# Spreading three of every four cache loads over later half blocks of TensorE work in a two-layer hybrid decoder step

## The chip, the cores and the metric

One core of one Trainium2 chip. The metric is the device time of one execution of the kernel in microseconds (us); of several runs the median counts.

## The reference, cut to what matters

Two layers of a hybrid decoder run over a prompt of 256 tokens and over 8 sample sequences of 4 tokens each, 288 token columns in all. Each layer is a half-step feed-forward network, a mixer of three branches with gates, and a second feed-forward network. The part that the change touches is the attention of the sample tokens into their own memory caches, in branch C:

```
x = LN1(alpha*x + 0.5*SwiGLU_1(x))
z = x @ w_in                                   # splits into cv, cb, cc, lx, lg, q and three gates
s = einsum('bthd,bmhd->bhtm', q, k_mem) / sqrt(128)      # sample b has its own k_mem[b], v_mem[b]
o = einsum('bthd,bmhd->bthd', softmax(s), v_mem)         # 256 memory tokens, 4 heads of 128
merged = g0 * (A @ conv_out) + g1 * (B @ lru_out) + g2 * (o @ att_out)
x = LN2(alpha*x + merged @ w_o)
x = LN3(alpha*x + 0.5*SwiGLU_2(x))
```

For each layer there are 8 key caches and 8 value caches, of 512 KB each, in HBM.

## The kernel before, in words

All data is float32. Each weight is cut into blocks of 1024 x 256 (1 MB) or 512 x 256 (512 KB). SyncE loads block n into one half of the buffer `raw` (n mod 2); it may do so when `lo_ready` says that both halves of block n-2 have been split. ScalarE casts the block to its high part `whi` (the helper `hi`, L735, recorded at L733), VectorE computes the rest `wlo` (the helper `lo`, L1036, recorded at L1030), each in two half blocks, and TensorE multiplies three times for each pair of 128-wide tiles (`stream`, L443, recorded at L439 to L441): a block of 1 MB is 48 matmuls of 288 columns, one of 512 KB is 24. After each half of a block TensorE raises `pe_half` by one, so `pe_half` = 2(n+1) says that block n is done.

The order of the work is written out by hand for each engine. The mixer's gated part of a layer is 24 blocks, from block number B on: for each of three branches b and each i of 0 to 3, a gate block `gate(b, i)` (number B+8b+2i, 1 MB out of `w_in`), and then a projection block `project(b, i)` (number B+8b+2i+1, 512 KB out of `conv_out`, `lru_out` or `att_out`).

Between these blocks TensorE does the sample attention in groups of four samples: the scores of samples 0 to 3 stand behind gate(0,1) (block B+2), those of 4 to 7 behind gate(0,3) (B+6), the values of 0 to 3 behind project(1,1) (B+11), those of 4 to 7 behind project(1,3) (B+15). The functions are `sample_scores` (L617, matmul L623) and `sample_values` (L627, matmul L631). Each sample raises `kv_used` by one.

GpSimd (POOL) issues the cache loads. There are four buffers `kv[0]` to `kv[3]`, two of them in the tensor `kv_more` and two within `pool`; load b (0 to 7 keys, 8 to 15 values) goes to buffer b mod 4, and from b = 4 on waits until sample b-4 has been used. The loop also has two other jobs: behind load 3 it clears `qz`, and behind load 11 it waits for the first prompt probabilities (`p_prob`) and clears the two `pz` tiles (L422), into which VectorE then copies the sample probabilities (L1463):

```
for b in range(2 * NS):
    if b == 2:
        pool_e.wait_ge(conv_done, l + 1)
    if b >= BATCH:
        pool_e.wait_ge(kv_used, l * (2 * NS) + b - BATCH + 1)
    ...
    g.dma_start(kv[b % BATCH], cache).then_inc(kv_in[b % BATCH], 16)
```

Other lines that the prediction's steps touch: `gate_lo` (L1375) is VectorE's split of the gate block after the next one; `branch_y` (L1378) drains a projection and splits the projection block after it; L1406, L1410, L1412 and L1413 are steps of the recurrent branch on VectorE; `prompt_values` (L649, matmul L654) needs the prompt probabilities that VectorE copied at L1466, behind the `pz` copies at L1463, and VectorE does these behind `gate_lo(1, 0, 0)`, the split of block B+10. L690 is the transpose of the sample probabilities, right behind gate(1,0).

Of the kernel before, what the change touches and what calls it, by code (L numbers as in the profile page):

```python
# [91 lines left out]
def hybrid_decoder_step(nc, I, O, dims):  # L92
# [20 lines left out]
    plan = Plan(L, KF, KB)  # L113
# [15 lines left out]
    with ExitStack() as ctx:  # L129
# [3 lines left out]
        def sem(name):  # L133
            return ctx.enter_context(nc.semaphore(name))
# [26 lines left out]
        KV, BATCH = AH * M, NS // 2  # L161
# [77 lines left out]
        hi_ready, lo_ready, pe_half, drained = sem("hi_ready"), sem("lo_ready"), sem("pe_half"), sem("drained")  # L239
# [138 lines left out]
        @block.gpsimd  # L378
        def _(pool_e):
            g = nc.gpsimd  # L380
            g.memset(ident[:, :], 0.0).then_inc(consts, 1)
            pool_e.wait_ge(consts, 1)
            g.affine_select(out=ident[:, :], in_=ident[:, :], compare_op=ALU.not_equal, fill=1.0, base=0,
                            pattern=[[-1, P]], channel_multiplier=1).then_inc(consts, 1)
            g.memset(ones[:, :], 1.0 / D).then_inc(consts, 1)
            for i, c in enumerate((4.0, 2.0, 4.0)):
                g.memset(eps[:, i:i + 1], EPS * c * c).then_inc(consts, 1)
            g.memset(junk[:, :], 1.0).then_inc(consts, 1)
            g.memset(bd[:, :, :, :], 0.0).then_inc(bd_zero, 1)
            pool_e.wait_ge(bd_zero, 1)  # L390
            pool_e.wait_ge(x_ready, KD)
            g.dma_start(pts[:, :, :], I["params"]).then_inc(pts_in, 16)

            pool_e.wait_ge(h_ready, 3)
            g.dma_start(sts[:, :, :, :], I["states"]).then_inc(sts_in, 16)
            g.dma_start(mem[:, :, :], I["mem"]).then_inc(mem_in, 16)
            for l in range(L):
                if l > 0:
                    pool_e.wait_ge(bd_psum, l * 8)
                for j, w in enumerate(("lru_wa", "lru_wx")):  # L400
                    for e in range(2):
                        h = P // 2
                        g.dma_start(bd[e * h:(e + 1) * h, j, :, e * h:(e + 1) * h],
                                    I[w][l].rearrange("(k e) a b -> e a k b", e=2)[e]).then_inc(bd_in, 16)
                pool_e.wait_ge(fill_out, plan.fills_done(l, "k"))
                g.dma_start(O["p_mem_k"][l], kt[:, :, :]).then_inc(k_out, 16)
                pool_e.wait_ge(fill_out, plan.fills_done(l, "v"))
                g.dma_start(O["p_mem_v"][l], vt[:, :, :]).then_inc(v_out, 16)

                for b in range(2 * NS):  # L410
                    if b == 2:
                        pool_e.wait_ge(conv_done, l + 1)
                    if b >= BATCH:
                        pool_e.wait_ge(kv_used, l * (2 * NS) + b - BATCH + 1)
                    cache = I["cache_k" if b < NS else "cache_v"][l, b % NS]
                    g.dma_start(kv[b % BATCH], cache).then_inc(kv_in[b % BATCH], 16)
                    if b == BATCH - 1:
                        g.memset(qz_flat, 0.0).then_inc(qz_zero, 1)
                    if b == NS + BATCH - 1:
                        pool_e.wait_ge(p_prob, l * AH + 1)  # L420
                        for t in pz_flat:
                            g.memset(t, 0.0).then_inc(pz_zero, 1)  # L422
                if l + 1 < L:
                    pool_e.wait_ge(kv_used, (l + 1) * (2 * NS))
                    g.dma_start(mem[:, :, :], I["mem"]).then_inc(mem_in, 16)
                pool_e.wait_ge(col_ready, l + 1)
                g.dma_start(O["cols"][l], cols[:, l]).then_inc(col_out, 16)

        @block.tensor
        def _(pe):  # L430
# [25 lines left out]
            def first_blocks(n):  # L456

                for s, k in ((s, k) for s in range(2) for k in range(KD)):
                    if (s, k) == (0, 0):
                        pe.wait_ge(xh_ready, 1)  # L460
                    elif s == 0:
                        pe.wait_ge(x_ready, k + 1)
                    if s == 0 and k % 2 == 0:
                        pe.wait_ge(lo_ready if k % 4 else first_lo, k // 4 + 1)
                    for h, (k0, _) in enumerate(halves(KD)):
                        if s == 1 and k == k0:
                            pe.wait_ge(lo_ready, 2 * (n + s) + h + 1)
                    for t in range(2):
                        out = ps[:, 2 * s + t, 0:T]
                        c = slice(t * P, (t + 1) * P)  # L470
                        mm(out, whi[:, s, k, c], xh[:, k, :], start=k == 0, stop=False)  # L471
                        mm(out, wlo[:, s, k, c], xh[:, k, :], start=False, stop=False)  # L472
                    if (s, k) == (0, 0):
                        pe.wait_ge(x_ready, 1)
                    for t in range(2):
                        last = mm(ps[:, 2 * s + t, 0:T], whi[:, s, k, t * P:(t + 1) * P], xl[:, k, :],
                                  start=False, stop=k == KD - 1)
                    if k in (KD // 2 - 1, KD - 1):
                        last.then_inc(pe_half, 1)
# [1088 lines left out]
```

## Time and profile before

| what | before |
|---|---|
| median of 3 runs | 1396.47 us (1395.02 to 1397.4) |
| the profiled execution's own time | 1396.84 us |
| its span, first to last instruction | 1394.9 us |
| TensorE (PE) busy | 98% of the span |
| VectorE (DVE), ScalarE (ACT), GpSimd (POOL) busy | 64%, 48%, 2% |
| granted TensorE clock | 0.998 |
| DMA | 243.60 MB, mean 175 GB/s |
| cache loads | 32 of 512 KB, on GpSimd's queue |
| loads of gate blocks and others out of `w_in` | 48 of 1 MB on SyncE's queue, 4.9 us median to landing |

A busy share says how much of the span an engine had an instruction running. "Landing" is the time from the issue of a transfer to its semaphore. The span leaves out 1.94 us of the execution's own time, at its two ends.

### The profile page before, as it was taken

What the parts mean: (1) busy time and instruction counts of PE and PEld (TensorE: products, weight loads), DVE (VectorE), ACT (ScalarE), POOL (GpSimd) and SP (SyncE); (2) the same over time, 40 slices, a digit from 0 to 9 for tenths busy, and PEclk for the clock granted to TensorE, in tenths of its full rate; (3) what the DMA queues carried; (4) which work ended last, traced back from release to release, by engine and by line L of the source; (5) the groups of instructions that cost most, each with busy time, mean ns of one, the idle gap of its engine ahead of it and who ended that gap; (6) DMA issues with size and microseconds to landing.
All of it is one profiled execution on the core that took longest, in us unless ns stands there. A gap on an engine that the chain in (4) does not pass through costs nothing.

```text
span 1394.9 us, 25447 instructions
## 1 busy us (share of the span) xinstructions
PE 1373.7 (98%) x10566; PEld 1357.2 (97%) x10566; DVE 894.8 (64%) x1180; ACT 665.9 (48%) x896; POOL 34.8 (2%) x68
## 2 busy tenths in 40 slices
PE   9999999999999999999999999999999999999996
PEld 8999999999899999999999999999998999999996
DVE  5555568496865885554685555585887568655444
ACT  5444446445444664444474444463544455544433
POOL 0100000000101000000000000000001000000000
PEclk9999999999999999999999999999999999999999
DMA  6654444755555454444445544446455453554441
GB/s 241 203 178 157 152 166 160 258 179 178 203 191 204 159 182 157 173 154 162 167 167 181 179 154 143 166 172 228 167 202 204 162 200 129 181 180 153 171 166 57
DMA packets 39998, 243.60 MB, mean 175 GB/s; under 512 B 4577, under 2 KB 4593, under 8 KB 16369
## 3 DMA queue, kind: packets, MB, share of 16 engines
q1 hardware_dynamic: 33264, 219.00, 45.0%
q0 software_dynamic: 5936, 22.01, 4.3%
q10 hardware_dynamic: 720, 1.47, 0.3%
q8 instruction: 59, 0.97, 0.3%
q14 instruction: 19, 0.15, 0.0%
HBM read 238.97 MB, written 3.50 MB: 174 GB/s over the span
## 4 chain that ended last, share of the span: by engine, by line
PE 91%; DVE 4%; DMA 3%; ACT 1%; issue 1%; DVEq 0%
PE ps L440 29%; PE ps L439 29%; PE ps L441 29%; DMA raw<-in_w_in 2%; DVE wlo L1030 1%; PE ps L527 1%; ACT whi L733 1%; PE ps L638 1%; PE ps L631 1%; PE ps L654 1%; PE ps L599 0%; PE ps L623 0%; DMA raw<-in_ffn_wg 0%; PE ps L471 0%; PE ps L472 0%
## 5 line engine op out<-in xcount | busy, mean ns | idle before, releaser
L1030 DVE TENSOR_TENSOR wlo<-raw,whi 128x1024 fp32r<-128x1024 f32 (+1 forms) x450 | 510.1, 1141 | 320.6 <-ACT whi L733 316.4
L733 ACT CAST whi<-raw 128x1024 fp32r<-128x1024 f32 (+1 forms) x446 | 437.2, 987 | 505.1 <-PE ps L441 382.9
L439 PE MATMUL ps<-xh,whi 128*128 128x288 f32 (+1 forms) x2144 | 635.6, 296 | 4.4 <-DVE wlo L1030 3.2
L440 PE MATMUL ps<-xl,whi 128*128 128x288 f32 (+1 forms) x2144 | 631.4, 294 | 0.0
L441 PE MATMUL ps<-xh,wlo 128*128 128x288 f32 (+1 forms) x2144 | 630.5, 294 | 0.0
L439 PEld LDWEIGHTS ps<-xh,whi 128*128 128x128 f32 x2144 | 404.4, 189 | 6.9 <-ACT pool L964 2.9
L440 PEld LDWEIGHTS ps<-xl,whi 128*128 128x128 f32 x2144 | 406.1, 189 | 0.7
L441 PEld LDWEIGHTS ps<-xh,wlo 128*128 128x128 f32 x2144 | 405.5, 189 | 0.0
L439 PE MATMUL ps<-hh,whi 128*128 128x288 f32 (+1 forms) x1088 | 322.0, 296 | 0.0
L440 PE MATMUL ps<-hl,whi 128*128 128x288 f32 (+1 forms) x1088 | 319.4, 294 | 0.0
L441 PE MATMUL ps<-hh,wlo 128*128 128x288 f32 (+1 forms) x1088 | 319.1, 293 | 0.0
L440 PEld LDWEIGHTS ps<-hl,whi 128*128 128x128 f32 x1088 | 206.1, 189 | 0.4
L439 PEld LDWEIGHTS ps<-hh,whi 128*128 128x128 f32 x1088 | 205.2, 189 | 1.2 <-issue 0.8
L441 PEld LDWEIGHTS ps<-hh,wlo 128*128 128x128 f32 x1088 | 205.7, 189 | 0.0
L1100 DVE SCALAR_TENSOR_TENSOR pool<-pool,ps 128x576 f32<-128x576 f32 x41 | 30.9, 753 | 49.9 <-ACT pool L774 49.9
L774 ACT ACTIVATE pool<-ps 128x576 f32<-128x576 f32 x41 | 26.7, 651 | 69.9 <-PE ps L441 69.9
L1106 DVE TENSOR_TENSOR pool<-pool,ps 128x576 f32<-128x576 f32 x44 | 33.1, 753 | 34.6 <-PE ps L441 34.6
L1030 DVE TENSOR_TENSOR hl<-pool,hh 128x576 f32 (+3 forms) x54 | 45.2, 844 | 0.9 <-ACT hh L819 0.2
L1146 DVE SCALAR_TENSOR_TENSOR y<-x,ps 128x576 f32<-128x576 f32 x18 | 13.6, 754 | 33.6 <-PE ps L441 33.6
L791 ACT CAST hh<-pool 128x576 f32 (+1 forms) x44 | 29.7, 675 | 3.2 <-DVE pool L1106 3.2
L860 ACT ACTIVATE xh<-y,pts 128x288 fp32r<-128x288 f32 x40 | 20.4, 532 | 18.9 <-DVE y L1221 18.4
L964 ACT ACTIVATE pool<-ps 128x576 f32<-128x576 f32 x24 | 15.6, 650 | 18.6 <-PE ps L441 18.6
(191 smaller groups left out, 747.5 us busy)
## 6 DMA issues: line engine op xcount, KB each, us to landing
raw<-in_w_in SPq DMA_DIRECT2D x48, 1024.0 KB, 4.9
raw<-in_ffn_wg SPq DMA_DIRECT2D x43, 1024.0 KB, 4.9
raw<-in_ffn_wu SPq DMA_DIRECT2D x43, 1024.0 KB, 4.9
raw<-in_ffn_wd SPq DMA_DIRECT2D x32, 1024.0 KB, 4.9
raw<-in_ffn_wd SPq DMA_DIRECT2D x16, 768.0 KB, 4.1
raw<-in_w_o SPq DMA_DIRECT2D x8, 1024.0 KB, 4.9
raw<-in_w_k_mem SPq DMA_DIRECT2D x4, 1024.0 KB, 5.5
raw<-in_w_v_mem SPq DMA_DIRECT2D x4, 1024.0 KB, 5.7
```

Source lines behind the costliest of these rows:

```text
L439: mm(out, wh, mh, start=start, stop=False)
L440: mm(out, wh, ml, start=False, stop=False)
L441: return mm(out, wl, mh, start=False, stop=stop)
L527: return mm(ps[:, 4 + kind, 0:T], ones[:, :], tile, start=first, stop=last)
L733: s_.copy(whi[:, s, k0:k1, :], raw[:, s, k0:k1, :]).then_inc(hi_ready, 1)
L774: s_.activation(th[:, :, :], ps[:, 0:2, 0:T], ACT.Tanh, scale=0.5).then_inc(ffn_tanh, 1)
L791: s_.copy(hh[:, bass.ds(i * 2, 2), :], hf[:, :, :]).then_inc(ffn_hi, 1)
L860: return s_.activation(out[:, k, :], y[:, k, :], ACT.Identity, bias=pts[:, l, bc + k:bc + k + 1])
L964: s_.activation(tg[:, :, :], ps[:, 0:2, 0:T], ACT.Tanh, scale=0.5).then_inc(gate_tanh, 1)
L1030: return v.tensor_tensor(out, full, high.bitcast(F32), sub)
L1100: v.scalar_tensor_tensor(sg[:, :, :], th[:, :, :], 1.0, ps[:, 0:2, 0:T], add, mult).then_inc(drained, 1)
L1106: v.tensor_tensor(hf[:, :, :], sg[:, :, :], ps[:, 2:4, 0:T], mult).then_inc(drained, 1)
```

## The change

For loads b = 5, 6, 7, 9, 10, 11, 13, 14, 15 of each layer, GpSimd waits for one more condition before it issues the load: that TensorE has reached a certain half block, counted by `pe_half`. Loads 4, 8 and 12 are issued as before. In each group of four the second load waits until the projection block behind the next place is done, the third for half of the gate block after it, the fourth for the other half. Nothing is taken out.

```
+                def spread(b):
+
+                    n = plan.at[l]["B"] + (2, 6, 10)[b // BATCH - 1]
+                    return 2 * n + (0, 4, 5, 6)[b % BATCH]
+
                 for b in range(2 * NS):
                     if b == 2:
                         pool_e.wait_ge(conv_done, l + 1)
                     if b >= BATCH:
                         pool_e.wait_ge(kv_used, l * (2 * NS) + b - BATCH + 1)
+                        if b % BATCH:
+                            pool_e.wait_ge(pe_half, spread(b))
                     cache = I["cache_k" if b < NS else "cache_v"][l, b % NS]
                     g.dma_start(kv[b % BATCH], cache).then_inc(kv_in[b % BATCH], 16)
```

## Rows read from the trace of the kernel before

**Rows 1.** The page: busy time of TensorE, and the chain that ended last.

```profile
PE 1373.7 (98%) x10566; PEld 1357.2 (97%) x10566; DVE 894.8 (64%) x1180; ACT 665.9 (48%) x896; POOL 34.8 (2%) x68
PE 91%; DVE 4%; DMA 3%; ACT 1%; issue 1%; DVEq 0%
```

**Rows 2.** Waits of TensorE, whole span: us in total, times, longest us.

```profile
PE ps L439 <- DVE wlo L1030: 3.2, 2, 2.7
```

**Rows 3.** Chain that ended last, layer 0, from 344 us: start, us, what.

```profile
344.79 7.77 DMA raw<-in_w_in
...
352.58 1.05 ACT whi L733
...
353.73 1.24 DVE wlo L1030
```

**Rows 4.** Timeline of GpSimd, layer 0: start, us, what, idle before and releaser.

```profile
338.68 1.05 POOL L416 DMA_DIRECT2D kv_more<-in_cache_k  x2 [36.73 <-PE ps L623]
...
362.56 1.05 POOL L416 DMA_DIRECT2D kv_more<-in_cache_v  x2 [21.79 <-PE ps L623]
...
373.89 1.84 POOL L422 MEMSET pool<- 128x1024 f32 x2 [9.23 <-DVE pool L1457]
391.82 1.05 POOL L416 DMA_DIRECT2D kv_more<-in_cache_v  x2 [16.09 <-PE ps L631]
```

**Rows 5.** Landing, us, of loads issued at 344.79, 1030.46, 1054.71, 333.31, 369.86.

```profile
raw<-in_w_in SPq DMA_DIRECT2D x1, 1024.0 KB, 7.8
...
raw<-in_w_in SPq DMA_DIRECT2D x1, 1024.0 KB, 6.9
...
raw<-in_w_in SPq DMA_DIRECT2D x1, 1024.0 KB, 6.3
...
raw<-in_w_in SPq DMA_DIRECT2D x1, 1024.0 KB, 6.0
...
raw<-in_w_in SPq DMA_DIRECT2D x1, 1024.0 KB, 4.8
```

**Rows 6.** Timeline of SyncE's queue: the loads of gate blocks B+10 and B+16, layer 0.

```profile
369.86 0.33 SPq L325 DMA_DIRECT2D raw<-in_w_in  x1
...
403.12 0.33 SPq L325 DMA_DIRECT2D raw<-in_w_in  x1
```

**Rows 7.** Stretches: length; PE, PEld, DVE, ACT, POOL busy (count); clock; DMA share; GB/s.

```profile
344.00:352.00 8.00, 8.00 (x64) 8.00 (x63) 7.97 (x8) 0.00 (x0) 0.00 (x0) 1.00 0.79 293
...
362.00:364.00 2.00, 2.00 (x34) 1.14 (x24) 1.63 (x2) 1.78 (x3) 1.44 (x3) 1.00 0.14 51
364.00:366.00 2.00, 2.00 (x15) 1.95 (x14) 1.51 (x5) 0.57 (x2) 0.65 (x2) 1.00 1.03 385
```

**Rows 8.** Timeline of VectorE, layer 0: the steps that bound an early landing.

```profile
351.35 0.81 DVE L1413 TENSOR_SCALAR pool<-pool 128x1248 f32<-128x1248 f32 x1
...
376.91 0.48 DVE L1463 COPY pool<-ps 128x128 f32<-128x128 f32 x2
377.31 0.68 DVE L1466 COPY pool<-ps 128x512 f32<-128x512 f32 x1
```

**Rows 9.** Timeline of TensorE, layer 0: gate(0,2), project(0,3), L690 and prompt_values(0) start.

```profile
342.81 0.29 PE L439 MATMUL ps<-xh,whi 128*128 128x288 f32 x1
...
364.24 0.48 PE L439 MATMUL ps<-hh,whi 128*128 128x288 f32 x1
...
373.92 0.38 PE L690 MATMUL ps<-ident,pool 128*128 128x128 f32 x2
...
378.14 1.10 PE L654 MATMUL ps<-pool,vt 128*128 128x256 f32 x4 [0.22 <-DVE pool L1466]
```

**Rows 10.** Timelines of TensorE and ScalarE, layer 1: the same three places.

```profile
1039.92 0.37 PE L439 MATMUL ps<-xh,whi 128*128 128x288 f32 x1 [0.45 <-DVE wlo L1030]
...
1061.07 1.05 ACT L733 CAST whi<-raw 128x1024 fp32r<-128x1024 f32 x1 [5.83 <-DMA raw<-in_w_in]
...
1064.51 1.10 PE L654 MATMUL ps<-pool,vt 128*128 128x256 f32 x4 [1.72 <-DVE pool L1466]
```

## The prediction

> **What bounds the kernel now.** I read the page first. TensorE is busy 98% of the span and makes up 91% of the chain that ended last [rows 1]. So a change in when GpSimd issues a load can only move the 21 us in which TensorE stands still, and of those only what lies beside cache loads. Next the waits of TensorE: it waited twice for a `wlo` split, 3.2 us in all, once for 2.7 us [rows 2]. The chain tells where: in layer 0 the gate block B+6 was issued at 344.79 and took 7.77 us to arrive; then a cast of 1.05, a split of 1.24 that ended at 354.97, and only then could TensorE start gate(0,3) [rows 3]. Layer 1 has the same wait with 0.45 us [rows 10]. The other waits near the loads are at `prompt_values(0)`: 0.22 us in layer 0 [rows 9], 1.72 in layer 1 [rows 10], behind the split of block B+10.
>
> Then the landings. An undisturbed 1 MB load out of `w_in` takes 4.8 us, B+6 took 7.8 in layer 0 and 6.9 in layer 1, B+10 6.3 in layer 1 and 4.8 in layer 0 [rows 5]. B+4 took 6.0 with no cache load near, so not all lateness comes from these. GpSimd issued four cache loads from 338.68, 362.56 and 391.82 on [rows 4]; after the second of these the queues moved 51 GB/s until 364 and 385 GB/s after it [rows 7]: 0.1 MB, or 0.3 us at the full rate, before 364, so the data starts some 1.2 us after the issue. 512 KB at 385 GB/s is 1.36 us, a group of four some 5.5 to 7 us. The first group flows from about 340 to 347, into the start of B+6's load; the second from 363.7 to about 370.5, just before B+10's, issued at 369.86 [rows 6].
>
> **Where the change puts each load.** Half a gate block is 24 matmuls, as many as a projection block. From gate(0,2)'s start at 342.81 to the split that gate(0,3) waited for (354.97, less 2.7 of waiting) are 72 of them in about 9.5 us [rows 2, 3, 9], so a step is about 3.15 us. project(0,1) ends where gate(0,2) begins. In layer 0:
> Load 4 stays. Load 5 is issued at 342.9 and flows 344.1 to 345.5. Load 6 is issued at 346.0 and flows 347.2 to 348.6. Load 7 is issued at 349.1 and flows 350.3 to 351.7. They are needed behind gate(0,3), two steps after 355, at about 361, so they are in time by over 5 us.
> Load 8 stays. project(0,3) starts at 364.24 [rows 9], so load 9 is issued at 367.5 and flows 368.7 to 370.1; load 10 at 370.7, flowing 371.9 to 373.3; load 11 at 373.9, flowing 375.1 to 376.5. They are needed at about 391, where TensorE frees the first of that group's buffers [rows 4].
> Load 13's condition is already met when load 12's is, because the values of samples 0 to 3 stand behind project(1,1). From 391.82 on [rows 4], loads 14 and 15 come some 5 and 8 us later, at 397 and 400, and flow until about 403, where the next `w_in` load is issued [rows 6]. They are needed two pairs of blocks behind 391.82, six steps or 19 us later, at about 411. I cost this group at nothing in both layers; the cover is some 8 us of slack, and if it went each late us would be one of TensorE.
>
> **B+6, layer 0.** Its load flows from about 346 to 349.3 when nothing is in its way. Now it has the tail of four loads before it; then it has the whole of load 6 in its middle, and load 5 only just ahead. Bounds for its landing: 4.8 us as if alone, or 7.8 as now and, if a whole cache load costs that much again, up to 9.1. I take 4.8 + 1.36 = 6.1, all of one cache load in its way, since the undisturbed row and the price per load are both measured at this place. It lands at 350.9, its cast ends at 352.0. But VectorE is busy for 7.97 of the 8 us to 352 [rows 7] with work that doesn't depend on this load, and its L1413 ends at 352.16 [rows 8]. Only then can the split start, 1.55 us earlier than 353.73. So of 2.73 us of wait, 1.2 stay whatever the load does: **-1.5 us**.
>
> **B+6, layer 1.** The load took 6.9 us for a wait of 0.45; at 6.1 the wait is gone: **-0.45 us**. It can't be more.
>
> **B+10, layer 0.** The second group now lies in a hole of SyncE's queue. After the change load 10 flows within this load's 371 to 374.3: 4.8 + 1.36 = 6.1 us. Behind it on the engines' queues stand ScalarE's cast, VectorE's split, the `pz` copies at 376.91 and the copy L1466, and TensorE waits for that already, by 0.22 us [rows 8, 9]. So all of it shows: **+1.3 us**. Bounds: 0 if the queues share without harm, +3.0 if it lands as late as B+6 does now.
>
> **B+10, layer 1.** It took 6.3 us [rows 5] though the second group was all but through. With load 10 in its way it takes 6.1 if the present lateness was chance, 6.3 + 1.36 if it was not. I take **-0.1 us**, bounds -1.4 (it lands in 4.9) and +1.5 (it lands in 7.8).
>
> **The `pz` clearing.** GpSimd's two memsets stand behind load 11 and now start at 373.89 for 1.84 us [rows 4]. With the change GpSimd waits for the end of gate(1,0) first, just before L690 at 373.92 [rows 9], and issues load 11, half of 1.05 us: the memsets end at about 376.35 instead of 375.73, still 0.55 us before VectorE copies at 376.91. Hidden in both layers; if VectorE came earlier, it would cost at most the 0.6 us of delay in each layer.
>
> Nine more semaphore waits per layer on GpSimd (2% busy) cost nothing. Loads 7 and 11 flow beside the 512 KB projection loads B+7 and B+11; these are used one block later, 6 us on, and 1.36 us more are covered.
>
> **Sum:** -1.5 - 0.45 + 1.3 - 0.1 = -0.75 us. The profiled execution took 1396.84 us, so it would take 1396.1; it stands 0.4 above the median, so I expect a median of 1395.7 us. No change that can be told: about 0.2%, or 2.8 us, is what a measurement of this kernel can tell from none.
>
> The queues' sharing deserves a second look. B+6's load got 3.0 and 2.0 us late from a burst that overlapped only its start [rows 5]. The Trainium skill, "DMA: Bandwidth & Descriptors", section "Queues, rings and completion order", says that each DMA engine takes turns between its queues, packet by packet. By that rule load 10 would give way to half of B+10's packets and cost 0.65 us instead of 1.36, and the sum would be about -2.1 us; the measured lateness of 2 to 3 us is more than taking turns explains.
>
> **Rivals.**
> *Clean sharing, faster.* The lateness came from the bursts' length, and a single 512 KB load hardly hurts. Then B+6 gives 1.55 and 0.45, B+10 in layer 0 costs nothing, and in layer 1 it lands in 4.9 instead of 6.3, giving 1.4: -3.4 us, 1393.1. For it: the only very late loads were beside bursts. Against: B+4 was 6.0 without one, and a MB and a half must pass at about 385 GB/s in any case. The middle way, -2.1 us, still counts as no change. Chance of faster by over 0.2%: 0.10.
> *Collision at B+10, slower.* What makes a load late is any cache load in flight with it, long or short; each costs the 2 to 3 us seen at B+6. Then B+6 gains nothing, B+10 lands in 7.8 in both layers: +3.0 and +1.5, together +4.5 us, 1401.0. It decides from the point where a collision costs more than 2.2 us at each of the two B+10 loads with nothing won at B+6, or less if B+6 gets worse. For it: VectorE's `pz` copies stand behind that split, and the second group was well placed before. Against: B+10 in layer 0 began while the second group's tail was flowing and still landed in 4.8. Chance of slower by over 0.2%: 0.17.
> *The loads don't move.* If the waits were already met, nothing would change and the time were 1396.5. By the block numbers that holds for load 13 alone. It falls within "same" with the forecast, which has 0.73 with it.
>
> **Numbers.** The forecast's own bounds are about -2.1 to +2.5. To leave out no more than 2 in 10, I go to most of the faster rival and to near the slower one: 1392.9 to 1400.0.
>
> **What the changed profile would show.** GpSimd's timeline has single cache loads about 3.1 us apart in the first two groups, and the third as two, one, one. B+6 lands in about 6.1 us in both layers, and VectorE's split for gate(0,3) starts right behind L1413; TensorE's wait there is 1.2 in layer 0 and none in layer 1. B+10 lands in 6.1 us, and `prompt_values(0)` waits about 1.5 us in both. The memsets start about 0.6 us later and nobody waits for them. The prediction is wrong if B+10's landing stays at 4.8 or goes beyond 7, if B+6's does not fall, or if a new wait of over 1 us shows at a place not named here.

## The result, and the profile after

The changed kernel takes 1399.37 us (median of 9 runs, 1398.57 to 1403.48) against 1395.16 us of the kernel before (9 runs). The ratio is 1.0036, with a 95% interval of 1.0026 to 1.0046: slower by 0.36%; the medians are 4.2 us apart. I had forecast no change: the median lies inside my range, but the forecast of no difference was wrong. The profiled execution took 1401.3 us with a span of 1399.3, 4.4 us over that of before. Line numbers above L415 are 7 higher than in the kernel before: L1473 is the old L1466, L661 the old L654.

GpSimd's timeline of the changed kernel, layer 0: start, length, what, count, idle time before and its releaser.

```profile
338.97 0.53 POOL L423 DMA_DIRECT2D kv_more<-in_cache_k  x1 [36.73 <-PE ps L630]
343.82 0.53 POOL L423 DMA_DIRECT2D kv_more<-in_cache_k  x1 [4.33 <-PE ps L448]
346.96 0.53 POOL L423 DMA_DIRECT2D pool<-in_cache_k  x1 [2.60 <-PE ps L448]
350.09 0.53 POOL L423 DMA_DIRECT2D pool<-in_cache_k  x1 [2.61 <-PE ps L448]
362.60 0.53 POOL L423 DMA_DIRECT2D kv_more<-in_cache_v  x1 [11.98 <-PE ps L630]
368.33 0.53 POOL L423 DMA_DIRECT2D kv_more<-in_cache_v  x1 [5.21 <-PE ps L448]
371.46 0.53 POOL L423 DMA_DIRECT2D pool<-in_cache_v  x1 [2.60 <-PE ps L448]
374.60 0.53 POOL L423 DMA_DIRECT2D pool<-in_cache_v  x1 [2.61 <-PE ps L448]
375.12 1.86 POOL L429 MEMSET pool<- 128x1024 f32 x2
```

The change did what it says: where there were bursts of four [rows 4], there are single loads 3.14 us apart, each released by TensorE. Now the waits of TensorE, whole span (total, times, longest):

```profile
PE ps L661 <- DVE pool L1473: 5.5, 2, 3.2
...
PE ps L446 <- DVE wlo L1037: 2.5, 1, 2.5
```

The wait for splits was 3.2 us [rows 2] and is 2.5: of the two only layer 0's is left. The wait at `prompt_values(0)` was 0.22 and 1.72 us [rows 9, 10]; it is 2.24 and 3.22. The landings of the loads of B+6 (issued at 345.21 in layer 0, 1032.52 in layer 1) and B+10 (369.91, 1056.06), in that order:

```profile
raw<-in_w_in SPq DMA_DIRECT2D x1, 1024.0 KB, 7.4
...
raw<-in_w_in SPq DMA_DIRECT2D x1, 1024.0 KB, 4.9
...
raw<-in_w_in SPq DMA_DIRECT2D x1, 1024.0 KB, 6.7
...
raw<-in_w_in SPq DMA_DIRECT2D x1, 1024.0 KB, 7.8
```

Against 7.8, 6.9, 4.8 and 6.3 [rows 5]. The chain that ended last runs through B+10's load in both layers; here is layer 1's (start, length, what):

```profile
1056.06 7.80 DMA raw<-in_w_in
...
1063.88 1.05 ACT whi L740
...
1066.10 0.48 DVE pool L1470 x2
1066.58 0.61 DVE pool L1473
...
1067.33 1.43 PE ps L661 x4
1068.76 1.71 PE ps L645 x4
```

The last two lines are slower than their work: in layer 0 of the same trace they are 1.10 and 0.86. The stretches from 1066 us on (columns as in [rows 7]) say why; the number behind POOL's is TensorE's granted clock:

```profile
1066.00:1068.00 2.00, 0.67 (x3) 0.65 (x4) 2.00 (x5) 1.55 (x3) 0.00 (x0) 0.99 0.07 29
1068.00:1070.00 2.00, 2.00 (x7) 1.56 (x6) 2.00 (x4) 0.37 (x1) 0.00 (x0) 0.50 0.45 74
1070.00:1072.00 2.00, 2.00 (x12) 1.91 (x11) 1.96 (x5) 0.00 (x0) 0.00 (x0) 0.66 0.89 369
```

Behind the wait of 3.22 us the clock was at 1.2 instead of 2.4 GHz for 3.4 us. At half pace that costs an estimated 1.7 us: 7 and 12 matmuls started in two stretches where the following one of this trace has 17. In the mixers of the kernel before the clock is 1.00 throughout.

The 4.4 us between the two spans are thus accounted for: B+6 -0.2 (2.73 to 2.52) and -0.45, B+10 +2.0 and +1.5, clock +1.7, together +4.6.

### The profile page after: what moved, and what is told of

The parts are those of the page before. It is cut to its first block, busy times and chain, and to the rows that moved or that the text cites. A ratio compares the mean times of both kernels' runs of the same rounds, so it can differ in the third digit from the quotient of the medians.

```text
span 1399.3 us, 25465 instructions
## 1 busy us (share of the span) xinstructions
PE 1375.3 (98%) x10566; PEld 1358.6 (97%) x10566; DVE 894.9 (64%) x1180; ACT 666.0 (48%) x896; POOL 35.4 (3%) x68
## 4 chain that ended last, share of the span: by engine, by line
PE 94%; DVE 3%; DMA 1%; issue 1%; ACT 0%; DVEq 0%
PE ps L447 30%; PE ps L446 30%; PE ps L448 30%; DMA raw<-in_w_in 1%; DVE wlo L1037 1%; PE ps L534 1%; PE ps L645 1%; PE ps L606 1%; PE ps L661 1%; PE ps L638 1%; PE ps L630 1%; PE ps L478 0%; DMA raw<-in_ffn_wg 0%; PE ps L479 0%; PE ps L483 0%
```

## The experiments

Theory C: cache loads issued close to B+10's load make it late, and the loss is there. Twelve runs follow: ten kernels, and one more trace of each of the two above. The edits are against the changed kernel unless it says otherwise. "Against before" is the ratio to the kernel before in runs on the same chip, with its 95% interval.

**Group two at once, groups one and three spread** (`e1_group2_at_once`).

```
-                        if b % BATCH:
+                        if b % BATCH and b // BATCH != 2:
```

> The changed kernel, but loads 9, 10 and 11 are issued at once as before; groups one and three stay spread. Theory C (collision): the 3.6 us of new waiting at prompt_values(0) come from cache loads issued around the load of gate block B+10. Then B+10 lands in 4.8 to 6.3 us again in both layers, the wait at the matmul of prompt_values falls from 5.5 us to about 1.9 or less, and the time is at or some 0.5 to 2 us under the kernel before. Rival R (the lateness of B+10 is chance, or the extra waits themselves cost time): B+10 lands in 6.7 and 7.8 as in the changed kernel and the time stays 3 to 5 us above the kernel before.

Measured: 1.0017 (1.0007 to 1.0027), median 1397.35 against 1395.78. B+10 landed in 4.8 and 6.4 us, and the waits of TensorE are:

```profile
PE ps L661 <- DVE pool L1473: 2.2, 2, 1.9
...
PE ps L446 <- DVE wlo L1037: 0.7, 1, 0.7
```

So the 3.6 us of new waiting belong to the second group: C's main claim holds, and R falls. In this trace (1394.51 us, the fastest of its 12 runs) the kernel is even ahead. But the median is 1.6 us over the kernel before, which C had not said.

**Group two alone** (`e2_group2_alone`; `if b % BATCH and b // BATCH == 2:`).

> The kernel before, but loads 9, 10 and 11 are spread as in the change; groups one and three are issued at once. Theory C: all of the loss is here, so 3 to 5 us slower than the kernel before, with some 5.5 us of waiting at prompt_values and 3.2 us of waiting for the split of B+6. Rival R: half or less of the loss, since two thirds of the added waits are gone.

Measured: 1.0038 (1.0025 to 1.0051), 1401.34 us. B+10 landed in 6.5 and 8.0, and `prompt_values` waited 5.3 us:

```profile
PE ps L661 <- DVE pool L1473: 5.3, 2, 3.4
```

A third of the added waits gives the whole loss. The half clock lasted 6.8 us in layer 1 of this trace, behind a wait of 3.41 us. The wait for B+6 was only 1.6 us with the burst in place (it landed in 5.9): that number moves by itself.

**The two kernels once more, one trace each** (`e3_before_again`, `e4_after_again`, no edit).

> The kernel before, unchanged, for a second trace. Theory C: B+6 lands in about 7 to 8 us in layer 0 and 7 in layer 1, B+10 in 4.8 in layer 0 and 4.8 to 6.3 in layer 1. Rival R (chance): the landings differ from the first trace by 2 us or more.

> The changed kernel, unchanged, for a second trace. Theory C: B+10 lands in 6.5 to 8 us in both layers again and prompt_values waits about 5.5 us in all. Rival R: at least one of the two lands near 4.8.

Measured, before again: B+6 7.2 and 7.0, B+10 4.9 and 6.2. Changed kernel again: B+6 6.5 and 4.9, B+10 5.8 and 7.1, `prompt_values` waiting 3.8 us in all, 2.49 of it in layer 1, again followed by 3.4 us of half clock. C holds in kind and misses in size: layer 0's B+10 at 5.8 is under its bound of 6.5, and the waits are 3.8 us instead of about 5.5; the lateness varies by 1 us from run to run. The rival had at least one of the two near 4.8, and neither is. The spans of these two traces are only 1.5 us apart, 1395.4 and 1393.9, where the same sum gives +3.1 (B+6 -0.1 and -0.4, B+10 +1.0 and +0.85, clock +1.7). The changed kernel was 2.0 us ahead already at B+4 in layer 0, before any load that was moved (its load was issued at 332.29 against 334.32), so two single traces can differ by 2 us for other reasons. The first pair happened to be level there (333.60 against 333.31), and only so could its sum come out.

**Groups one and three, each alone** (`e5_group1_alone`, `e6_group3_alone`; `b // BATCH == 1` or `== 3`).

> The kernel before with only loads 5, 6 and 7 spread. Theory C: the load of B+6 lands in 4.9 us in layer 1 (6.9 before), so its wait of 0.3 to 0.45 us goes; in layer 0 it lands in 5.7 to 7.4 instead of 7.2 to 7.8, and the wait of 1.8 to 2.7 us falls by 0 to 1.5. Median 0.5 to 2 us under the kernel before. Rival S (spreading costs something of its own in every group): at or over the kernel before, by some 1.5 us as in the run with groups one and three.

> The kernel before with only loads 13, 14 and 15 spread. Theory C: within 1 us of the kernel before; the only w_in load that it can touch is the one issued some 3 to 4 us after load 15, or that of the next block in layer 1 (5.8 to 6.3 us instead of 5.2), where TensorE has slack. Rival S: 1 us or more slower, and the run with groups one and three got its 1.6 us here.

Measured: 1.0005 (0.9994 to 1.0016) and 1.0009 (1.0000 to 1.0018). Group three costs next to nothing, as costed. Group one gains nothing, against C: B+6 landed in 5.6 and 4.9 and its waits were 0.8 us in all instead of 2 to 3. What was won was given back later, in layer 1: gate block B+8's load was issued at 1038.8, now only 3.5 us behind load 7, and landed in 6.8 us (5.0 before). TensorE waited 0.23 us within that block and 0.35 us behind it, which it doesn't in the kernel before. B+10 landed in 6.5, and the clock fell to half behind a wait of 2.17:

```profile
1053.59 0.40 PE L446 MATMUL ps<-xh,whi 128*128 128x288 f32 x1 [0.23 <-DVE wlo L1037]
...
1063.56 1.10 PE L661 MATMUL ps<-pool,vt 128*128 128x256 f32 x4 [2.17 <-DVE pool L1473]
```

**Load 10 on ScalarE's queue** (`e7_load10_on_scalar_queue`). The same load at the same half block, issued by another engine; TensorE waits for it on a semaphore of its own. Load 9 stays where the changed kernel has it, on GpSimd's queue.

```
+                    if b == 10:
+                        continue
```

That is in GpSimd's loop; in ScalarE's program, behind the first prompt exponentials:

```
+                    if i == 0:
+                        act.wait_ge(kv_used, l * (2 * NS) + 7)
+                        act.wait_ge(pe_half, 2 * (B + 6) + 5)
+                        s_.dma_start(kv[2], I["cache_v"][l, 2]).then_inc(kv10_in, 16)
```

> The changed kernel, but load 10, the one that falls into the flow of B+10's load, is issued by ScalarE's queue at the same half block, not by GpSimd's. Theory B (bytes: 512 KB more in flight make B+10 late): B+10 lands in 5.5 to 8 us in both layers, as in the changed kernel, and prompt_values waits 3.8 to 5.5 us in all. Theory G (it is the issue by GpSimd, whose data in the changed kernel flowed only when B+10's was nearly through, that slows the other queue): B+10 lands within 0.6 us of the kernel before (4.8 and 6.3).

Measured: 1.0030 (1.0014 to 1.0047); B+10 landed in 7.4 in layer 0 and 6.3 in layer 1, waits 4.7 us. Layer 0 speaks against theory G: the queue doesn't matter there. Layer 1 gives what the kernel before has, as G said. Neither theory has both, so the run is inconclusive; the load was issued 1.16 us behind B+10's in layer 0 and 1.0 in layer 1, not the 1.6 of the changed kernel, and load 9 stood 1.5 to 1.6 us ahead in both. It adds one thing: here the clock fell in layer 0, behind a wait of 2.8 us.

**Load 9 ahead, loads 10 and 11 late** (`e8_load9_ahead_only`), **and load 9 early too** (`e9_loads10_11_late`).

```
-                    return 2 * n + (0, 4, 5, 6)[b % BATCH]
+                    return 2 * n + (0, 4, 6 if b // BATCH == 2 else 5, 6)[b % BATCH]
```

In the second, the entry for load 9 is 0 as well.

> The changed kernel, but load 10 of the second group waits as long as load 11 does, so only load 9 stands near the load of B+10, issued 1.6 us ahead of it, and loads 10 and 11 come 4.7 us behind its issue. If load 10, issued into B+10's flow, does the harm: B+10 lands in 4.8 to 5.5 us and the wait at prompt_values falls to 2 us or less. If load 9, ahead of it, does: 6 to 8 us as in the changed kernel, and the wait stays 3.8 to 5.5 us.

> The changed kernel, but in the second group load 9 is issued at once with load 8, and loads 10 and 11 wait for the end of gate(1,0), when B+10's load has nearly landed. No cache load starts in the 5 us ahead of it or in its flow. If any cache load near it makes it late: B+10 lands in 4.8 to 5.2 us in both layers, in layer 1 too, where it took 6.3 in the kernel before behind the burst of four, and the wait at prompt_values falls to 0.5 us or less. If B+10's lateness in layer 1 has nothing to do with the cache loads: 6.3 us there and a wait of 1.6 to 1.9. Time: the clock's drop in layer 1 goes with the wait; within 1 us of the kernel before, or under it.

Measured: 1.0036 (1.0021 to 1.0050) and 1.0016 (1.0007 to 1.0025). In the first, B+10 landed in 6.5 and 5.7, in the second in 5.0 and 6.0; `prompt_values` waited 3.2 and 2.6 us. In layer 0 the two kernels differ in nothing but load 9, issued 1.55 us ahead of B+10's load or with load 8, and that is worth 1.5 us: **in layer 0 a cache load issued just ahead is enough**; none needs to be issued behind it. For layer 1, 5.7 against 6.0 says nothing; in the first kernel load 9 was 2.9 us ahead of B+10's load there. With load 10 on ScalarE's queue, load 9 was 1.6 us ahead in layer 1 and B+10 took no longer than in the kernel before, so this is shown for layer 0 only. And in layer 1 B+10 takes 6.0 us with no cache load near, against my expectation: that part of the lateness isn't the cache loads'. In both traces B+8 in layer 1 was late too (6.9 and 6.2), 3.5 us behind load 7.

**Matmuls in the wait** (`e10_filled_wait`).

```
                     if i == 0:
+                        for _ in range(16):
+                            mm(ps[:, 4, 0:T], xh[:, 0, 0:P], xh[:, 0, :], start=True, stop=True)
                         pe.wait_ge(pz_ready, MT * (l + 1))
```

> The changed kernel with 16 matmuls of 288 columns more (2.1 us), whose result nothing reads, where TensorE stands still before prompt_values(0), in both layers. Theory K (part of the loss is TensorE's clock, which the traces of the changed kernel show at half for 3.4 us right behind this wait in layer 1): no half clock there, the blocks from B+12's load to B+14's take 10.2 us again in layer 1 instead of 11.9, and the time is 1 to 2 us under the changed kernel's, some 2 to 3.5 us above the kernel before, though work was added. Rival (the clock's drop has another cause, or costs nothing): as slow as the changed kernel or slower, 4 to 6 us above the kernel before.

Measured: 1.0023 (1.0013 to 1.0033), 1399.17 us against 1395.56. The trace has no half clock in the mixers, and the blocks run at full pace behind the place, here beside the line above from 1068 us on:

```profile
1068.00:1070.00 2.00, 2.00 (x17) 2.00 (x16) 0.84 (x4) 1.02 (x4) 0.00 (x0) 1.00 0.94 352
```

The ratio is below the changed kernel's though 2.3 us of work was added per layer, as K said, but the two intervals overlap, so for the time it is a hint. For the trace it isn't clean either: in layer 1 B+10 landed in 4.8 us, so there was no wait to fill, and no clock drop to prevent; in layer 0 B+10 was late (7.0), but there the changed kernel has no drop to prevent. That filling the wait keeps the clock up is not shown. The landing of 4.8 says something else: load 9 was issued 2.9 us ahead of B+10's load and load 10 0.24 us behind it, and neither made it late; the instruction packet came ahead of the flow (below).

**A candidate: only the last loads late** (`e11_last_loads_late`), against the kernel before.

```
+                    if b == 2 * BATCH - 1:
+                        pool_e.wait_ge(pe_half, 2 * (plan.at[l]["B"] + 2) + 6)
+                    if b == NS + BATCH - 1:
+                        pool_e.wait_ge(p_prob, l * AH + 1)
+                        for t in pz_flat:
+                            g.memset(t, 0.0).then_inc(pz_zero, 1)
                     cache = I["cache_k" if b < NS else "cache_v"][l, b % NS]
                     g.dma_start(kv[b % BATCH], cache).then_inc(kv_in[b % BATCH], 16)
...
-                    if b == NS + BATCH - 1:
-                        pool_e.wait_ge(p_prob, l * AH + 1)
-                        for t in pz_flat:
-                            g.memset(t, 0.0).then_inc(pz_zero, 1)
```

> A candidate built on the kernel before: only load 7 waits, for the end of gate(0,2), and load 11 is issued behind the pz memsets instead of ahead of them; all other loads are issued at once. If a burst's length is what reaches into B+6 and B+10: B+6 lands in 4.8 to 6.2 us in both layers, its waits fall from 3.2 us to 1.2 or less, B+10 lands in 4.8 to 5 in both layers and prompt_values waits 0.5 us or less; 2 to 3.5 us under the kernel before. If the nearness of any cache load counts (load 6 still ends just where B+6's begins): B+6 stays at 6.5 to 7.5 in layer 0 and the gain is 1 to 2 us.

Measured: 1.0007 (0.9998 to 1.0017), 1396.70 us: no gain. B+6 landed in 5.9 and 6.6, with a wait of 1.4 us in layer 0, and B+10 in 5.0 and 6.5. Three loads instead of four in the burst leave B+10 in layer 1 as late as it was: the burst's length is not its cause.

**Thirty-two small matmuls more at the start** (`e12_forty_warm`), against the kernel before.

```
-WARM_NARROW, WARM_WIDE = 8, 8
+WARM_NARROW, WARM_WIDE = 40, 8
```

> The kernel before with 40 instead of 8 narrow matmuls (8 columns) at its very start, where TensorE waits for its first data anyway; nothing else is changed, no cache load moves. It tests the rest of the lateness. In the traces so far a load out of w_in lands in 4.8 us where no packet of the instruction queue (16 KB, some 0.95 us on one DMA engine) falls into its flow, and in 6.0 to 6.3 where one does: B+4 in layer 0 and B+10 in layer 1, in every trace of the kernel before. With 32 more instructions pairs in TensorE's program these packets come some 3 to 4 us earlier against the blocks. Theory I (instruction fetch): the landings of B+4 in layer 0 and B+10 in layer 1 fall to about 4.8 to 5.2, and prompt_values waits 0.5 us or less in layer 1 instead of 1.6 to 1.7; another load may become late instead. Rival (these two loads are late for another reason, fixed by their place in the program): both stay at 5.6 to 6.3. Time: 0 to 2 us under the kernel before if no other load is hit.

Measured: B+4 in layer 0 landed in 4.9 us (6.0 before), B+10 in layer 1 in 4.9 (6.3), and `prompt_values` waited 0.5 us in both layers together. As the expectation allowed, another load became late: B+4 in layer 1 took 6.6 (4.9 before), with a packet in its last 2 us, and behind it TensorE waited 1.5 us for B+6's split instead of 0.45. An instruction packet is one transfer of 16 KB on the queue that the profile calls "instruction". The DMA queues of the kernel before while B+10's data flowed in layer 1, 1055.7 to 1060.5 us (packets, MB, share):

```profile
q1 hardware_dynamic: 256, 1.46, 83.5%
q8 instruction: 1, 0.02, 1.2%
```

The same flow in this kernel, 1062.6 to 1066.5, has no instruction packet:

```profile
q1 hardware_dynamic: 196, 1.24, 86.1%
q0 software_dynamic: 3, 0.01, 1.3%
```

Theory I holds for both loads. The fourteen traces bear it out elsewhere as well. Of the 1 MB loads out of `w_in` with nothing issued by GpSimd or ScalarE from 9 us ahead to 5.5 us behind, the 30 in which such a packet starts 1 to 3.8 us behind the issue landed in 5.5 to 6.8 us (median 6.0). The 252 with no packet from 1 us ahead to 4 us behind landed in 4.7 to 6.6 (median 4.85), three of them above 5.4. The time of this kernel is 1.0031 (1.0020 to 1.0043), slower: I had the 32 matmuls covered by the wait for the first data, and they were not. The kernel before starts its first real matmul at 7.21 us, this one later:

```profile
3.12 10.58 PE L436 MATMUL ps<-hh 128*128 128x8 f32 x48 [3.12 <-DVE hh L1041]
13.49 0.44 PE L471 MATMUL ps<-xh,whi 128*128 128x288 f32 x1
```

6.3 us were lost at the start of this trace and 4.1 in the median (1399.79 against 1395.65), so by an estimate some 2 us were won behind it; by the two spans (1400.3 and 1394.9) it is 0.9. A padding with the same effect and no cost wasn't tried.

## Why the prediction was wrong

**What bounds the kernel, where each load goes, the third group, the `pz` clearing**: right. The loads of the first two groups were issued within 1 us of the instants worked out; loads 14 and 15 came 2.6 and 2.8 us later than those, 2.0 of it from B+10's lateness. The memsets ended at 376.98, two us before VectorE came for them at 378.89. The slower rival named the place and the mechanism: B+10's landing, shown whole by the wait at `prompt_values(0)`. It had 0.17, because I priced a collision at 1.36 us. That its 1401.0 us is so near the profiled 1401.3 is luck: it had B+10 in layer 0 at +3.0 and no clock term.

**The steps that failed.** Of the terms of my sum:

*B+10, layer 0, +1.3:* it was +2.0, and +1.0 in the second pair of traces; a size that was off by less than a microsecond either way.

*B+10, layer 1, -0.1:* it was +1.5 and +0.9. I had let the present lateness of 6.3 us be "chance" that the new load would replace. It goes with the instruction packet in its flow: it is there, at 5.7 us or more, in all twelve traces in which the packet starts 1 to 4.1 us behind the load's issue, and gone in the two in which it doesn't, at 4.8 and 4.9. The cache loads' lateness comes on top: 6.3 became 7.8, and 7.1 and 8.0 in the two other traces with loads 9 and 10 where the change puts them, though not with load 10 on ScalarE's queue (6.3).

*B+6, layer 0, -1.5:* it was -0.2 and -0.1. The split could have started 1.55 us earlier, but the load landed in 7.4 and 6.5 us where I said 6.1. This one varies most: 5.2 to 7.4 in the eight traces with the group spread, mean 6.2, and 5.8 to 7.8 in the five with the burst of four, mean 6.8. So 6.1 was right on average, and the 7.8 that I read as the present state was its upper end. The waits of TensorE there are 1.4 us on average with the group spread and 1.5 with the burst: there was hardly anything to win.

*B+6, layer 1, -0.45:* right, 4.8 or 4.9 us and no wait, in all eight traces with that group spread. But the move put load 7 3.5 to 3.7 us ahead of B+8's load in layer 1, a term that I had not looked at: B+8 landed in 6.2 to 6.9 us in four of these eight traces and in 5.0 to 5.5 in the others (4.8 to 5.2 without the move), and TensorE waited 0.3 to 0.7 us for it in those four. In all eight an instruction packet started 0.1 to 0.6 us behind the issue, so that isn't what tells them apart.

*Missing:* TensorE's clock, +1.7 us. No term had it, since no row of before in this part shows it at half.

In the first pair of traces the misses are 0.7 + 1.6 + 1.3 + 1.7 = 5.3 us, which takes my -0.75 to +4.55.

**The price per collision.** I took the time of the bytes, 512 KB at 385 GB/s. The stretch from 372 to 373 us, in B+10's flow in layer 0, of the kernel before and then of the changed one:

```profile
372.00:373.00 1.00, 1.00 (x10) 1.00 (x9) 1.00 (x2) 0.00 (x0) 0.00 (x0) 1.00 0.99 418
```

```profile
372.00:373.00 1.00, 1.00 (x10) 1.00 (x9) 1.00 (x2) 0.00 (x0) 0.00 (x0) 1.00 0.99 213
```

The DMA engines are busy all of it in both, and move half as much in the second. (From 371.3 to 375 us they move 360 and 249 GB/s, at a share of 0.93 and 0.80.) It isn't the other load's bytes that fill the time: from 371.7 to 374.9 us GpSimd's queue has no packet, the data of load 10, issued at 371.46, began at 375.0, and it took 7.7 us to land. So my 1.36 us is refuted as the price here. In the clean comparison in layer 0 it is 0.9 to 2.5 us: 6.5 with load 9 ahead alone and 5.8 to 7.4 with load 10 as well, against 4.8 to 5.0 in the eight traces without either. The Trainium skill ("DMA: Bandwidth & Descriptors", "Queues, rings and completion order") says that a DMA engine takes turns between its queues by packets. The 0.65 us that I had estimated from that rule is refuted as the price as well, but the rule isn't at odds with the trace: where both queues had data in flight, from 376 to 378 us, they ran 98 and 112 packets.

**What stays open.** Why a load 1.6 us ahead does harm in layer 0. A burst of four that ended just where B+10's data began did none there; load 9 alone, ending there as well, did. B+6 in layer 1, with a cache load issued 0.1 us behind it and another at 3.2, landed in 4.9 each time, and B+10 in layer 1 of the filled kernel in 4.8 with one at 0.24. So neither bytes nor nearness alone decide. The distance of the issues may matter, but it doesn't decide alone either: at the same distances B+10 in layer 0 took 5.8 to 7.0, B+8 in layer 1 5.0 to 6.9. Open too is why spreading one and three together costs 0.17% in the median while the trace of its fastest run shows less waiting. B+8's lateness in layer 1, which that trace doesn't have and others do, would do part of it, and a clock that falls in some runs and not in others would do the rest, but only one execution of each kernel was profiled.

## What to carry to other kernels

A transfer that is moved out of a burst isn't free where it arrives: ask first whether the burst lies in a hole of the other queue, as the second group did, and leave it there; then list every load that each moved transfer now comes close to, as load 7 did to B+8's. Price a collision from several measured landings with and without it, not from bytes over bandwidth and not from one trace: B+6's load in layer 0 landed in 5.8 to 7.8 us with the same burst ahead of it. Before calling a late landing chance look at what else is in its flow, instruction packets included. Where TensorE is the bound, a wait of 2 to 3 us can cost another 1.7 us in clock.

## What the runs showed of the hardware

An instruction packet (16 KB, in these stretches one per 16 us on average, 10 to 22 us apart) went with a lateness of 0.7 to 1.7 us of the 1 MB load in whose flow it fell: B+4 in layer 0 took 5.5 to 6.5 us and B+10 in layer 1, with no cache load issued near it, 6.0 to 6.5, and 4.9 each when the packets were shifted. In 30 other loads with a packet starting 1 to 3.8 us behind the issue the landing was 5.5 to 6.8 us, in 252 without one 4.85 in the median.

TensorE's clock fell to half for 3.4 us behind waits at `prompt_values(0)` of 2.17, 2.49, 2.8 and 3.22 us, and for 6.8 us behind one of 3.4. It did not behind waits of 1.62 to 1.93 us at that place, nor, in layer 0, behind 2.24 us there and 2.73 us at gate(0,3).
